# Down product of the feed-forward by seven block products a quarter, its result by tokens

## The reference

```python
def rmsnorm(x, g):
    x32 = x.astype(jnp.float32)
    y = x32 * lax.rsqrt(jnp.mean(x32 * x32, axis=-1, keepdims=True) + EPS)
    return y.astype(x.dtype) * g

h2 = rmsnorm(x, pre_norm_mlp[l])
y = jnp.square(jax.nn.relu(h2 @ w_up[l])) @ w_down[l]
x = x + rmsnorm(y, post_norm_mlp[l])
```

## Time and profile before

| | us |
|---|---|
| median of 3 runs | 953.04 (952.84 to 953.87) |
| profiled execution, span from first to last instruction | 951.7 |
| what the median has beyond that span | 1.3 |
| TensorE busy | 943.3 |
| VectorE busy | 587.3 |
| ScalarE busy | 417.5 |
| POOL busy | 100.4 |

### The profile page before, as it was taken

How to read it: one execution, slowest core, us unless ns; L and a number is a source line. 1 busy time by engine, 2 the same in 40 slices (tenths; PEclk the granted TensorE clock), 3 DMA queues, 4 the chain that set the end, 5 groups by cost and what they waited for, 6 DMA issues and landing times.

```text
span 951.7 us, 13474 instructions
## 1 busy us (share of the span) xinstructions
PE 943.3 (99%) x5234; PEld 774.8 (81%) x5234; DVE 587.3 (62%) x1062; ACT 417.5 (44%) x773; POOL 100.4 (11%) x109
## 2 busy tenths in 40 slices
PE   9999999999999999999999999999999999999998
PEld 7779777778898777777778889988888888888887
DVE  6668759898658788765656625863244344445545
ACT  6465346455645456444553234562342233212332
POOL 2004204321220000000002212000000000000021
PEclk9999999999999999999999999999999999999999
DMA  7322121122325112121222442353233322323102
GB/s 246 110 69 67 46 67 67 46 67 78 113 70 196 60 64 67 53 72 38 86 67 89 127 161 70 121 187 113 89 108 92 108 89 89 110 89 92 42 1 89
DMA packets 25918, 85.99 MB, mean 90 GB/s; under 512 B 2944, under 2 KB 5952, under 8 KB 25600
## 3 DMA queue, kind: packets, MB, share of 16 engines
q1 hardware_dynamic: 25040, 80.45, 26.1%
q10 hardware_dynamic: 576, 4.36, 1.2%
q0 software_dynamic: 240, 0.33, 0.1%
HBM read 80.93 MB, written 4.19 MB: 89 GB/s over the span
## 4 chain that ended last, share of the span: by engine, by line
PE 86%; DVE 8%; ACT 2%; issue 1%; DMA 1%; SPq 0%; DVEq 0%; ACTq 0%
PE PB L418 13%; PE PB L420 13%; PE PB L419 13%; PE PB L1010 5%; PE PB L1008 5%; PE PB L1009 5%; PE PB L648 4%; PE PB L685 3%; PE PB L663 2%; DVE wl L1504 2%; PE PB L888 2%; PE PB L890 2%; PE PB L889 2%; PE PB L459 2%; PE PB L463 2%; PE PB L458 2%
## 5 line engine op out<-in xcount | busy, mean ns | idle before, releaser
L418 PE MATMUL PB<-hh,wh 128*128 128x512 f32 x576 | 235.2, 408 | 0.0
L420 PE MATMUL PB<-hh,wl 128*128 128x512 f32 x576 | 224.8, 390 | 0.0
L419 PE MATMUL PB<-hl,wh 128*128 128x512 f32 x576 | 224.6, 390 | 0.0
L1504 DVE TENSOR_TENSOR wl<-raw,wh 128x1024 fp32r<-128x1024 f32 (+2 forms) x90 | 113.7, 1263 | 50.9 <-ACT wh L1048 50.5
L418 PEld LDWEIGHTS PB<-hh,wh 128*128 128x128 f32 x576 | 108.2, 188 | 28.2 <-issue 6.4
L420 PEld LDWEIGHTS PB<-hh,wl 128*128 128x128 f32 x576 | 108.1, 188 | 23.3
L419 PEld LDWEIGHTS PB<-hl,wh 128*128 128x128 f32 x576 | 108.3, 188 | 23.0 <-issue 2.2
L1048 ACT ACTIVATE wh<-raw 128x1024 fp32r<-128x1024 f32 (+2 forms) x90 | 91.3, 1018 | 53.4 <-PE PB L463 14.0
L1215 ACT ACTIVATE S<-S,sm 128x256 f32<-128x256 f32 (+3 forms) x96 | 50.6, 528 | 105.0 <-DVE sm L1607 80.8
L1504 DVE TENSOR_TENSOR wl<-AR,wh 128x1024 fp32r<-128x1024 f32 x55 | 67.6, 1230 | 40.4 <-ACT wh L1048 40.4
L1048 ACT ACTIVATE wh<-AR 128x1024 fp32r<-128x1024 f32 x55 | 57.8, 1052 | 71.0 <-PE PB L1010 71.0
(11 more groups left out here) (380 smaller groups left out, 1688.4 us busy)
## 6 DMA issues: line engine op xcount, KB each, us to landing
AR<-in_dne SPq DMA_DIRECT2D x32, 512.0 KB, 3.6
AR<-in_upe SPq DMA_DIRECT2D x24, 512.0 KB, 3.5
raw<-in_w2g SPq DMA_DIRECT2D x16, 512.0 KB, 3.4
raw<-in_w1e SPq DMA_DIRECT2D x10, 512.0 KB, 3.4
raw<-in_w1q SPq DMA_DIRECT2D x8, 512.0 KB, 3.4
raw<-in_woab SPq DMA_DIRECT2D x8, 512.0 KB, 3.5
raw<-in_w2e SPq DMA_DIRECT2D x5, 512.0 KB, 4.5
raw<-in_w1c SPq DMA_DIRECT2D x4, 512.0 KB, 3.4
```

The costliest lines, as they stand in the source:

```text
L418: e.matmul(bank[:], a[:, col(k)], xa[:, k, :], start=k == 0, stop=False)
L419: e.matmul(bank[:], a[:, col(k)], xb[:, k, :], start=False, stop=False)
L420: i = e.matmul(bank[:], b[:, col(k)], xa[:, k, :], start=False, stop=k == 7)
L1504: e.tensor_tensor(low_, raw_of(c), high.bitcast(F32), ALU.subtract).then_inc(*up("lo", c))
```

## The change

The down product of a quarter, 512 tokens by 1024 hidden features by 1024 results, is seen as two by two blocks: 256 tokens, 512 hidden features, 512 results. Seven products of sums and differences of blocks replace the eight products of blocks (Winograd's form of Strassen's method). The blocks of hidden features are the even and the odd tiles. In the order of `PRODUCTS` a product takes its tokens from a block itself (`b`) or from a sum of blocks (`t`), and its weights from one of four slots, `a` to `d`.

- Operands change places: 128 tokens are loaded, 512 columns of weights are streamed, and the result has tokens on its partitions. (A row of a matmul names the streamed operand first: `PB<-hh,wh` streams tokens, `PB<-wh,gh` weights.) A product is two pieces (chunks) of 12 matmuls each, and gives two banks.
- VectorE makes four sums of blocks of tokens for each pair of hidden tiles, in the PSUM banks 4 and 5 (`hidden`, L2144 to L2149), ScalarE their high halves (`mixed`, L1465), VectorE their low halves (L2159). The squares are now made by ScalarE alone.
- VectorE makes four sums of blocks of weights, two chunks each, in place in their slots: `third` and `second` in the up stretch, `first` and `fourth` in the down stretch. Slot `d` is loaded twice a quarter, once to be summed and once as it is.
- Each product's two banks are added over the quarters by VectorE (`added`, L2186). In quarter 3 the seven results are combined to the four blocks of the result as they come.
- The norm's factors stand by tokens at the end: the sum of squares comes from ScalarE's accumulation (`weight`), POOL multiplies by the gain (`YG`), TensorE transposes x in 32 pieces (`turned_x`), VectorE adds (`final`, L2235). The result is stored by tokens, in three pieces of 512 KB and two of 256.
- Up tiles use the banks 6 and 7 alone. Chunks of `w_up` come through the two buffers `raw`, where they came through eight places from quarter 1 on. The squares of x for the norm before the up product move from the up to the down stretch of quarter 0.

```diff
-        s += [("dne", 8 * q + i, NW) for i in range(8)]
+        s += [("dn", 14 * q + i, NW) for i in range(14)]
...
+PRODUCTS = (("b", 0, "a"), ("b", 1, "b"), ("t", 1, "d"), ("t", 0, "a"), ("t", 2, "c"), ("b", 2, "b"), ("t", 3, "d"))
+SUMMED = {2: "s2", 3: "s1", 4: "s3", 5: "s4"}
+RESULT = ((1, 6), (5, 3))
...
+        PS = [[ar(1024 * n + 512 * s, 512) for s in range(2)] for n in range(4)]
+        PS += [[ar(12288 + 1024 * n + 512 * s, 512) for s in range(2)] for n in range(2)] + [[acc[:], R[:]]]
+        SQ2, TT = PS[5], [PB[4], PB[5]]
+        th, tl = (x[:, :, :].rearrange("p (j i) t -> p j (i t)", i=2) for x in (gh, gl))
+        YG = [ar(4096, 1024), ar(5120, 1024), raw[1][:], ar(8192, 1024)]
+        POSTG = raw[0][:]
...
-                for m in range(8 if q < 3 else 4):
-                    c = CH["dne", 8 * q + m]
-                    a, b = wh[c % 3], wl[c % 3]
-                    bank, before = tenant(banks[turns % 7], *(("y0", m) if q == 0 else ("yy", q, m)))
-                    turns += 1
-                    e.wait_ge(*to("lo", c))
-                    e.wait_ge(*to(*before))
-                    for k in range(8):
-                        if m == 0:
-                            e.wait_ge(*to("ul", q, k))
-                        e.matmul(bank[:], a[:, col(k)], gh[:, k, :], start=k == 0, stop=False)
-                        e.matmul(bank[:], a[:, col(k)], gl[:, k, :], start=False, stop=False)
-                        i = e.matmul(bank[:], b[:, col(k)], gh[:, k, :], start=False, stop=k == 7)
...
+                for n in range(7):
+                    got = [tenant(2 * (n % 3) + s, *summed(q, n, s)) for s in range(2)]
...
+                    if n == 2:
+                        e.wait_ge(*to("tw", q, 3, 1))
+                    e.wait_ge(*to("lo", piece(q, n, 0)))
+                    if (q, n) == (3, 6):
+                        turned_x(2, 6)
+                        turned_x(3, 2)
...
+                        turned_x(0, 4)
+                        turned_x(1, 6)
+                        break
+                    for j in range(4):
+                        c = piece(q, n, j // 2)
+                        a, b, w = wh[c % 3], wl[c % 3], slice(512 * (j % 2), 512 * (j % 2) + 512)
+                        if j == 2:
+                            e.wait_ge(*to("lo", c))
+                        if n < 2:
+                            e.wait_ge(*to("bl", q, j, n))
+                        for s in range(2):
+                            bank, before = got[s]
+                            if j == 0:
+                                e.wait_ge(*to(*before))
+                            high, low = features(n, j, s)
+                            e.matmul(bank[:], high, a[:, w], start=j == 0, stop=False)
+                            e.matmul(bank[:], low, a[:, w], start=False, stop=False)
+                            x = e.matmul(bank[:], high, b[:, w], start=False, stop=j == 3)
+                        if j % 2:
+                            x.then_inc(*up("gemm", c))
...
+            def mixed(q, j):
+
+                e.wait_ge(*to("tc", q, j))
+                for x in range(2):
+                    e.activation(th[:, j, 512 * x:512 * x + 512], TT[x][:], ACT.Copy).then_inc(*up("th", q, j, x))
...
+                a, t = tmp[m % 4 - 1], [TT[i // 2][:, 256 * (i % 2):256 * (i % 2) + 256] for i in range(4)]
+                e.wait_ge(*to("uq", q, m))
...
+                e.tensor_tensor(t[0], a[:, 256:512], a[:, 0:256], ALU.subtract).then_inc(*up("tc0", q, j, 0))
+                e.tensor_tensor(t[2], b[:, 256:512], a[:, 256:512], ALU.subtract).then_inc(*up("tc0", q, j, 2))
+                e.wait_ge(*to("tc0", q, j, 0))
+                e.tensor_tensor(t[1], b[:, 256:512], t[0], ALU.subtract).then_inc(*up("tc0", q, j, 1))
+                e.wait_ge(*to("tc0", q, j, 1))
+                e.tensor_tensor(t[3], b[:, 0:256], t[1], ALU.subtract).then_inc(*up("tc", q, j))
+                e.wait_ge(*to("uh", q, j, 1))
+                e.tensor_tensor(bl[:, j, 256:768], b[:], bh[:, j, 256:768].bitcast(F32),
+                                ALU.subtract).then_inc(*up("bl", q, j, 1))
...
+                    e.wait_ge(*to("th", q, j, x))
+                    e.tensor_tensor(tl[:, j, t], TT[x][:], th[:, j, t].bitcast(F32), ALU.subtract).then_inc(*up("tw", q, j, x))
...
+                e.tensor_tensor(slot("c", jj), slot("a", jj), slot("c", jj), ALU.subtract).then_inc(*up("sc", q, "s3", jj))
...
+                e.wait_ge(*arrived("d", jj, q))
+                e.wait_ge(*to("sc", q, "s3", jj))
+                e.tensor_tensor(slot("d", jj), slot("d", jj), slot("c", jj), ALU.subtract).then_inc(*up("sc", q, "s2", jj))
...
+                e.wait_ge(*to("lo", piece(q, 0, jj)))
+                e.tensor_tensor(slot("a", jj), slot("d", jj), slot("a", jj), ALU.add).then_inc(*up("sc", q, "s1", jj))
...
+                e.wait_ge(*to("lo", piece(q, 1, jj)))
+                e.tensor_tensor(slot("b", jj), slot("b", jj), slot("d", jj), ALU.subtract).then_inc(*up("sc", q, "s4", jj))
...
+                if n == 0:
+                    e.wait_ge(*to("yv", 2, 1, s))
+                    sum_to(PS[1][s], bank, "yv", 3, 0, s)
+                    e.wait_ge(*to("yv", 2, 2, s))
+                    sum_to(PS[2][s], bank, "ye", 3, 0, s)
...
+                e.wait_ge(*(to("yv", 3, 0, s) if n == 1 else to("ye", 3, 0, s) if n == 2 else
+                            to("ye", 2, 3, s) if n == 3 else to("yv", 3, n - 2, s)))
+                sum_to(PS[n][s], bank, "ye", 3, n, s)
+                if n in (2, 3, 4):
+                    e.wait_ge(*to("ye", 3, n, s))
+                if n == 2:
+                    e.wait_ge(*to("ye", 2, 5, s))
+                    sum_to(PS[5][s], PS[2][s], "yv", 3, 1, s)
+                    e.wait_ge(*to("ye", 2, 4, s))
+                    sum_to(PS[4][s], PS[2][s], "yv", 3, 2, s)
+                if n == 3:
+                    e.wait_ge(*to("yv", 3, 1, s))
+                    sum_to(PS[5][s], PS[3][s], "yv", 3, 3, s)
+                if n == 4:
+                    sum_to(PS[3][s], PS[4][s], "yv", 3, 5, s)
+                    e.wait_ge(*to("ye", 2, 6, s))
+                    sum_to(PS[6][s], PS[4][s], "yv", 3, 4, s)
...
+                for n in range(14):
+                    if n > 1:
+                        added(q, n // 2 - 1, n % 2)
...
+                    c = CH["dn", 14 * q + n] + 2
+                    if c < len(PLAN):
+                        lo(c)
+                    if n == 1:
+                        mixed(q, 3)
+                    if n in (1, 2):
+                        first(q, n - 1)
+                    if n in (3, 5):
+                        fourth(q, (n - 3) // 2)
+            added(3, 6, 0)
+            for b in (2, 3):
+                for h in (1, 0):
+                    final(b, h)
+            added(3, 6, 1)
+            final(0, 0)
+            final(0, 1)
+            e.wait_ge(*to("ye", 3, 6, 1))
+            e.wait_ge(semaphore("postg"), 16)
+            e.tensor_tensor(YG[1][:, 512:1024], result(1, 1), POSTG[:, 512:1024], ALU.mult).then_inc(*up("yg1"))
+            final(1, 0)
+            final(1, 1)
...
+            e.wait_ge(*to("lo", piece(3, 4, 0)))
+            for b, h, *event in ((0, 0, "ye", 3, 1), (1, 0, "ye", 3, 1), (2, 1, "yv", 3, 5), (3, 1, "yv", 3, 5),
+                                 (2, 0, "ye", 3, 5), (3, 0, "ye", 3, 5), (0, 1, "ye", 3, 6)):
+                t = slice(512 * h, 512 * h + 512)
+                e.wait_ge(*to(*event, b % 2))
+                e.tensor_tensor(YG[b][:, t], result(b, h), POSTG[:, t], ALU.mult).then_inc(*up("yg", b, h))
...
+                for jj in range(2):
+                    e.wait_ge(*to("lo", piece(q, 2, jj)))
+                    e.wait_ge(*to("sc", q, "s1", jj))
+                    e.wait_ge(*to("sc", q, "s4", jj))
+                    load_down("d", jj, q, 1)
+                if q < 3:
+                    for name, n in (("a", 3), ("c", 4), ("b", 5), ("d", 6)):
+                        for jj in range(2):
+                            e.wait_ge(*to("lo", piece(q, n, jj)))
+                            load_down(name, jj, q + 1)
+                    for m in range(2, 8):
+                        load(upper(q + 1, m))
```

More of the change, by code:

```diff
@@ L327, in landed, with piece, upper, arrived @@
         def landed(c):
-            if c < FAR_AT:
-                return semaphore(f"raw{c % NR}"), 16 * (c // NR + 1)
-            return semaphore(f"far{(c - FAR_AT) % FAR}"), 16 * ((c - FAR_AT) // FAR + 1)
+            return semaphore(f"raw{NEAR[c] % NR}"), 16 * (NEAR[c] // NR + 1)
+        def piece(q, n, jj):
+            return CH["dn", 14 * q + 2 * n + jj]
+        def upper(q, m):
+            return CH["upk", 3] if (q, m) < (0, 4) else CH["upe", 8 * q - 4 + m]
+        def arrived(name, jj, q, again=0):
+            return semaphore(f"dn_{name}{jj}"), 16 * ((2 * q + again if name == "d" else q) + 1)
+        def summed(q, n, s):
```

(63 more changed lines are left out.)

402 lines of the change are left out of this document (209 added, 193 removed), and 14 rows, old and new, of the table SIGNALS.

## The result

The changed kernel takes 945.06 us (median of four runs, 943.74 to 946.46) against 952.96 for the kernel before in the same session: ratio 0.9915, 95% interval 0.9901 to 0.9929. It is faster by 7.9 us, under 1%, where 17.6 were forecast, and lies 2.1 us above the range. The four runs fall into two pairs: 943.74 and 943.85 with a mean granted clock of 0.996, 946.26 and 946.46 with 0.994. The profiled execution, 943.74 with a span of 942.4, is one of the first pair.

A forecast was written before the change was run, and what follows sets the result against it. TensorE bounds the kernel, its feed-forward matmuls without a hole. 951.7 − 16.3 (removed matmuls) + 1.7 (quarter 0 stall) − 3.0 (quarter 3 with the end) = 934.1, with 1.3 added 935.4 us; range 929.5 to 943.

The forecast's parts named there:

- Removed matmuls: Down product: eight tiles of 24 matmuls become seven products, 5.44 us less per quarter, 16.3 us in quarters 0 to 2.
- Rival (e): Matmuls with streamed weights have a pitch longer by 0.03 us, eating 20 us: result about 953; chance 0.01.
- VectorE's new work, quarters 1 and 2: VectorE's added sums and low halves fit: 28.5 of 43.5 us in the up stretch, 29.1 of 38.1 in the down.
- Quarters 1 and 2: Down stretches: VectorE's low halves come in time, as little as 0.5 us to spare; stall 0, bound 1.5 each.
- Nothing for: Terms costed at nothing: the DMA queue, and one fp32 matmul of sums replaced by four tiny ones, 0.
- Quarter 0: Late ScalarE and VectorE after the first four tiles: TensorE loses 1.7 us at the first down pieces, bounds 0 and 4.
- Quarter 3: Down stretch: VectorE's 22 sums and POOL hold the last product until 39.2 us; with the end, 3.0 us gained.
- I take 0.5 for each of four: Quarter 3's down stretch: each of POOL's four scalings slows VectorE by 0.5 us, moving 37.2 to 39.2.
- The reach of the last product: Quarter 3: TensorE would reach the last product at 32.6 us, or 34.2 with 16 transposes in front.
- The end: After the last matmul: sums, results, scaling to 49.1 us, then 3.0 for 1 MB of stores: end at 52.1, before 55.1.
- Rival (b): VectorE slower than its rows: stalls of 4, 1.5 and 1.5, last product 4 later: 944.7 us, from 940 on; chance 0.21.
- Rival (c): TensorE's clock falls to 1.2 GHz after standing in quarter 3; last product takes 5.4 us more: 940.8; chance 0.07.

The follow-up runs named there:

- the filled wait: Changed kernel with 18 unused matmuls in place of the wait before quarter 1's second up tile: up stretch 47.96 us, span 943.0.
- the earlier read: Changed kernel with VectorE's root(2), its read of bank 7, moved to piece 13 of quarter 0's down stretch: 939.48 us, ratio 0.9847.
- the four repairs: Changed kernel with root(2) earlier, other banks for up tiles (0,6) and (0,7), POOL later and first(q, 0) in the up stretch: 935.03 us, ratio 0.9807.

## Why the prediction was wrong

**Removed matmuls**: right. Two quarters are 5.50 us shorter each than before, against 5.44. (A piece whose tokens are a block itself has a pitch of 0.230, 11.04 us for 48 matmuls from 725.26 to 736.30; the others 0.227.) Rival (e) is gone.

**VectorE's new work, quarters 1 and 2**: right in the down stretches, to a tenth of a microsecond, with margins of 0.5 us that held. The four rows that write into a bank took 0.43, the low bound.

**The step that failed** is "Quarters 1 and 2 … I take 0 for both quarters", together with "Nothing for … One fp32 matmul of sums goes, four tiny ones come: 0". I took the sums of squares as work on TensorE alone and never asked which bank they stand in, who reads it and what stands ahead of the reader. The diff had both facts, `sums(2, 7)` and the up tiles' two banks. The cost was 6.06 us, shown by two kernels that each undo it, of which 1.6 is the clock, shown by the filled wait. This alone is most of the 8.3. The sums' own work on TensorE, taken at 0, was 0.8.

**Quarter 0**: the lateness was sized well (12.4 forecast, 12.1 measured), but the place was wrong: the late relu holds bank 6, and the third up tile needs it. Given another bank, the wait came at the third piece, as written. The cost: 2.1 in the up tiles and nothing at the piece, for 1.7.

**Quarter 3**: right in kind, mis-sized in one term. "I take 0.5 for each of four" of POOL's rows, 2.0 us, was 3.9. Without POOL the forecast was 37.2 and the kernel without it gave 37.03. In the earlier trace rows POOL's row, 909.09 to 910.39, covers only the first 0.4 us of VectorE's 1.48, and 0.25 of stretch from 0.4 of overlap is already more than half. The other row there, VectorE's 1.80 at 571.14, lies beside two of POOL's:

```profile
567.69 4.16 POOL L2152 TENSOR_TENSOR acc<-acc,tmp 128x512 f32<-128x512 f32 x3 [21.87 <-ACT tmp L1102]
572.15 1.94 POOL L2152 TENSOR_TENSOR acc<-acc,tmp 128x512 f32<-128x512 f32 x1 [0.30 <-ACT tmp L1102]
```

The one that was under way when VectorE began ends at 571.85: 0.57 of stretch from 0.71 of overlap. The one that began behind VectorE's is the longer one itself, 1.94 for 1.30. In quarter 3 the two conversions have 1.10 from 1.23 (923.38 to 924.61) and 1.09 from 1.22 (927.54 to 928.76). In all four VectorE loses the overlap with the POOL row that is under way when it begins, less 0.13 to 0.15 us. So the price of overlap was there to be read, and I took one row's stretch for the price of each row. The reach of the last product, 34.2 without VectorE, was 35.67: its first matmul comes 1.66 us behind the first transpose (1.6 forecast), so the twelve pieces in front took 34.0, where 32.6 was forecast. Of those 1.4 us 0.7 lie at the two waits of 0.2 and 0.2 in the pitch of 0.230; the rest stays open, and in the changed kernel all of it hid behind VectorE.

**The end**: 7.2 us from the product's last matmul forecast, 6.9 measured (935.5 to 942.4).

**The rivals.** Rival (b) named the right size, 944.7, and that is luck, for its mechanism was another: stalls of 1.5 in quarters 1 and 2 for a VectorE slower than its rows did not come, and rows into banks are no slower. Only its part for POOL came, 1.75 us of delay of the last product where it had 4. Rival (c), the clock, did happen, in another place and at a smaller price: I looked for it at the last product, at 5.4 us for all 24 matmuls, and it came behind the wait of quarter 1, eight matmuls, 1.6 us.

## What to carry to other kernels

Where a change takes banks or buffers away from a rotation, list for every one left each tenant with its last reader, and look at what stands ahead of that reader in its engine's order: a read of 0.15 us cost 6.06 here. Engines that are late in one place have nothing to give there, so a step that helps the late quarters may hurt the first; look at each quarter's margin before moving it in all. Where POOL and VectorE run side by side on two SBUF inputs each, cost nearly the whole overlap, not a fixed amount for each row.

## What the runs showed of the hardware

- **The clock falls behind short waits.** In the feed-forward part, after each of the four waits of 4.16 or 4.17 us that the profiles hold (the changed kernel, and those with the late tile's other bank, with POOL later, without the combining sums) about eight matmuls ran at 0.43 us a pitch, and so they did after the three of 2.2 to 2.3 (the earlier read, the filled wait, the four repairs); the execution of the four repairs with a mean clock of 1.000 suggests that it does not come each time). Of the waits of 1.76 to 1.83 us, in quarters 0 and 3, five of eleven were followed by such rows within 1.6 us; of those of 1.1 to 1.4 us none. Each slow stretch cost 1.6 us where TensorE set the pace and nothing where VectorE was later anyway. The Trainium skill's page TensorE: Matmul & The Clock Gate, section Part 1, has it that idleness lets the clock fall back, and the trace agrees. Why a wait of 1.8 us is followed by it in one execution and not in the next stays open; the two pairs of times of the changed kernel differ by 2.5 us at clocks of 0.996 and 0.994, which one or two such stretches more would give, but the slower pair has no profile, so that is argued and not shown.
- **POOL and VectorE nearly take turns.** Where both have two SBUF inputs, four rows of POOL lengthened VectorE's by 3.9 us and were longer themselves by 1.2 (6.33 against four of 1.29). For each of the single conversions the loss is what is left of the POOL row already under way, less 0.13 to 0.15 us.
